# A short convolution computed from matmul banks as they fill, and one weight block rounded ahead of the first attention softmax

## The reference, cut to what matters

```python
def _short_conv_branch(b_gate, c_gate, h, conv_w, w_out):
    S = h.shape[1]
    zp = jnp.pad(c_gate * h, ((0, 0), (CONV_K - 1, 0), (0, 0)))
    y = zp[:, 0:S] * conv_w[0]
    for k in range(1, CONV_K):
        y = y + zp[:, k:k + S] * conv_w[k]
    return (b_gate * y) @ w_out
...
def _mla_branch(q_lat, kv_lat, k_rope, qn_g, kvn_g, w_uq, w_ukv, w_out, pos):
    ...
    o = _blocked_causal_attention(q, k, v, (MLA_NOPE + MLA_ROPE) ** -0.5)
    return o.reshape(Bsz, S, MLA_HEADS * MLA_V) @ w_out
```

## Time and profile before

| | |
|---|---|
| three timed runs | 2857.13, 2850.22, 2849.24 us; median 2850.22 |
| the profiled execution | 2851.05 us, of which its span from first to last instruction is 2849.2 us |
| TensorE busy | 2691.5 us, 94% of the span |
| GpSimd busy | 2204.4 us, 77% |
| ScalarE busy | 1492.1 us, 52% |
| VectorE busy | 1368.2 us, 48% |
| mean granted TensorE clock | 0.979 |

### The profile page before, as it was taken

One profiled execution on the slowest core, in us unless ns is written; L12 is line 12 of the kernel. 1 busy time (PEld: TensorE's weight loads), 2 busy tenths in 40 slices (PEclk: granted clock), 3 DMA queues, 4 the chain that ended last, 5 costly groups with the idle time before them and its releaser, 6 DMA issues.

```text
span 2849.2 us, 60006 instructions
## 1 busy us (share of the span) xinstructions
PE 2691.5 (94%) x21756; PEld 2602.7 (91%) x21756; DVE 1368.2 (48%) x2509; ACT 1492.1 (52%) x2261; POOL 2204.4 (77%) x1681
## 2 busy tenths in 40 slices
PE   8999999999999999999989989999999899898997
PEld 8998988889999989988889989998999899788997
DVE  2125445656556554535556554346433533735334
ACT  4444555465455545456465554457545644555445
POOL 8876766757978967676758968978899699667994
PEclk9999999999999999999999999999999999999998
DMA  6554434434554545443434545544555455444552
GB/s 240 184 172 150 147 134 134 156 119 156 184 170 163 185 144 174 134 148 122 168 111 163 184 140 170 185 143 160 170 184 186 137 189 182 137 135 145 190 182 79
DMA packets 123283, 452.63 MB, mean 159 GB/s; under 512 B 13680, under 2 KB 13680, under 8 KB 122480
## 3 DMA queue, kind: packets, MB, share of 16 engines
q1 hardware_dynamic: 121104, 441.43, 46.4%
q10 hardware_dynamic: 2016, 8.91, 0.9%
HBM read 449.24 MB, written 1.05 MB: 158 GB/s over the span
## 4 chain that ended last, share of the span: by engine, by line
POOL 49%; issue 24%; PE 20%; DVE 4%; ACT 1%; POOLq 1%; DVEq 0%; ACTq 0%
POOL wl L373 26%; POOL wl L374 24%; PE R L408 4%; PE R L412 4%; PE R L411 4%; PE Y L408 1%; PE Y L411 1%; PE Y L412 1%; DVE M L2276 1%; PE R L571 0%; PE Y L648 0%; DVE G L2275 0%; ACT wh L1140 0%; POOLq L379 0%; DVE XLB L1915 0%
## 5 line engine op out<-in xcount | busy, mean ns | idle before, releaser
L373 POOL TENSOR_TENSOR wl<-raw,wh 128x512 fp32r<-128x512 f32 x836 | 1114.9, 1334 | 620.3 <-ACT wh L1140 614.1
L408 PE MATMUL R<-XHB,wh 128*128 128x256 f32 (+1 forms) x4168 | 1190.7, 286 | 28.5 <-POOL wl L374 16.7
L412 PE MATMUL R<-XHB,wl 128*128 128x256 f32 (+1 forms) x4168 | 1182.2, 284 | 0.0
L411 PE MATMUL R<-XLB,wh 128*128 128x256 f32 (+1 forms) x4168 | 1178.0, 283 | 0.0
L374 POOL TENSOR_TENSOR wl<-raw,wh 128x512 fp32r<-128x512 f32 x836 | 1140.8, 1365 | 0.0
L1140 ACT ACTIVATE wh<-raw 128x1024 fp32r<-128x1024 f32 x836 | 877.3, 1058 | 287.7 <-PE R L408 206.9
L408 PEld LDWEIGHTS R<-XHB,wh 128*128 128x128 f32 x4168 | 792.1, 190 | 36.4 <-POOL wl L374 23.2
L411 PEld LDWEIGHTS R<-XLB,wh 128*128 128x128 f32 x4168 | 795.2, 191 | 1.7 <-issue 1.0
L412 PEld LDWEIGHTS R<-XHB,wl 128*128 128x128 f32 x4168 | 793.7, 190 | 0.0
L408 PE MATMUL Y<-BH,wh 128*128 128x256 f32 x1408 | 398.0, 283 | 1.3 <-DVE BL L1839 1.3
L412 PE MATMUL Y<-BH,wl 128*128 128x256 f32 x1408 | 396.4, 282 | 0.0
(11 more groups left out here) (408 smaller groups left out, 3177.9 us busy)
## 6 DMA issues: line engine op xcount, KB each, us to landing
raw<-in_stream SPq DMA_DIRECT2D x836, 512.0 KB, 3.3
G<-in_wcmp ACTq DMA_DIRECT2D x2, 2048.0 KB, 7.6
G<-in_mem ACTq DMA_DIRECT2D x2, 1024.0 KB, 6.7
TB<-in_table SPq DMA_DIRECT2D x1, 1312.0 KB, 12.4
X<-in_x SPq DMA_DIRECT2D x2, 512.0 KB, 6.0
out_dram<-X ACTq DMA_DIRECT2D x4, 256.0 KB, 2.2
WS<-in_mix_w ACTq DMA_DIRECT2D x2, 256.0 KB, 7.8
PTS<-in_mix_b ACTq DMA_DIRECT2D x2, 256.0 KB, 7.6
```

The costliest lines, as they stand in the source:

```text
L373: pool.tensor_tensor(wl[:, s, 0:512], raw[:, r, 0:512], wh[:, s, 0:512].bitcast(F32), ALU.subtract)
L408: i = pe.matmul(o, wh[w], hi, start=start, stop=False, skip_group_check=True)
L411: pe.matmul(o, wh[w], lo, start=False, stop=False, skip_group_check=True)
L412: i = pe.matmul(o, wl[w], hi, start=False, stop=stop, skip_group_check=True)
```

## The change

VectorE now makes p = c * h and the three taps directly from the bank of each h chunk, with four instructions per chunk (`convolved`): p goes into the unused half of the same bank, and the taps go from there to `Z`. The bank is given back after the fourth. ScalarE no longer evicts chunks 22 to 25. Two of the four `convolved` calls stand ahead of the token mix in VectorE's list and two behind it; the 13 old instructions behind the compressed softmax are gone. On ScalarE, one `split_next` is moved from the last gate of the first pair (`split=u != 1`) to ahead of the first pair's softmax (`ahead=1`), in latent attention alone.

```diff
-            def attention_pairs(units, filler):
+            def attention_pairs(units, filler, ahead=0):
+                for _ in range(ahead):
+                    split_next()
                 for p in range(len(units) // 2 + 1):
...
                 def z(c):
                     split_next()
+                    if Z_CH <= c < Z_CB:
+                        skip(1)
+                        return
                     m, o = chunk()
...
-                def gate(b, c):
-                    split_next()
+                def gate(b, c, split=True):
+                    if split:
+                        split_next()
...
-                attention_pairs([mla_unit(h) for h in range(8)], lambda u: (gate(u // 4, 2 * u % 8), gate(u // 4, (2 * u + 1) % 8)))
+                attention_pairs([mla_unit(h) for h in range(8)], lambda u: (gate(u // 4, 2 * u % 8), gate(u // 4, (2 * u + 1) % 8, split=u != 1)), ahead=1)
...
-                skip(UP_CHUNKS - 8 + Z_N - Z_UP - 1)
-
+                skip(UP_CHUNKS - 8)
+
+                cv = lambda k, c: col(f"conv{l}", 4 * k + c)
+
+                def convolved(c):
+                    evicted(Z_CC + c)
+                    m, o = chunk()
+                    p, y = o[:, T:2 * T], Z[:, Z_CH + c, :]
+                    step(stt(p, o[:, 0:T], col(f"b_in{l}", Z_CH + c), Z[:, Z_CC + c, :], ALU.add, ALU.mult))
+                    step(ts_(y, p, cv(2, c), None, ALU.mult))
+                    step(stt(y[:, 1:T], p[:, 0:T - 1], cv(1, c), y[:, 1:T], ALU.mult, ALU.add))
+                    take(stt(y[:, 2:T], p[:, 0:T - 2], cv(0, c), y[:, 2:T], ALU.mult, ALU.add), m)
+
+                convolved(0)
+                convolved(1)
                 for g in range(4):
                     o = ready(f"mix{g}")
...
+
+                convolved(2)
+                convolved(3)
+                skip(Z_N - Z_CB)
...
-                cv = lambda k, c: col(f"conv{l}", 4 * k + c)
-                evicted(Z_CH + 3)
-                step(tt_(Z[:, Z_CC:Z_CC + 4, :], Z[:, Z_CC:Z_CC + 4, :], Z[:, Z_CH:Z_CH + 4, :], ALU.mult))
-                for c in range(4):
-                    p, y = Z[:, Z_CC + c, :], Z[:, Z_CH + c, :]
-                    step(ts_(y, p, cv(2, c), None, ALU.mult))
-                    step(stt(y[:, 1:T], p[:, 0:T - 1], cv(1, c), y[:, 1:T], ALU.mult, ALU.add))
-                    step(stt(y[:, 2:T], p[:, 0:T - 2], cv(0, c), y[:, 2:T], ALU.mult, ALU.add))
                 evicted(Z_CB + 3)
```

## The result

The changed kernel takes 2838.49 us in the median of 5 runs (2836.86 to 2841.61), the kernel before 2853.49 in the median of 5 on the same chip (2849.24 to 2857.13): ratio 0.9949 with a 95% interval of 0.9936 to 0.9962, faster by 0.5%. The profiled execution took 2838.49 us. The forecast was 2835.4 with a range of 2830 to 2843.

A forecast was written before the change was run, and what follows sets the result against it. TensorE, busy 94%, bounds the kernel, so only its stops give time back: 7.42 us in each of two mixers, 14.8 us off 2851.05, gives 2836.2, or 2835.4 us as the median; range 2830 to 2843.

The forecast's parts named there:

- The chain: Latent attention's first pair: VectorE's convolution, ScalarE's place in line, GpSimd's remainder, then TensorE, which waits 5.22 us.
- The sum: First pair's four gate chunks, 18.99 us to 11.57: 5.22 of wait, 2.0 clock, 0.2 start; two mixers, 14.8 us.
- The new instructions: Sixteen VectorE instructions on banks, 2.1 us a chunk, 8.4 a mixer, ending ahead of the compressed scores at no cost.
- ScalarE's part: Rounding ahead of latent attention's first softmax ends at 359.2, delays exponentials 0.7 us, and readies the fourth gate block at 363.2.
- Slack 3 us: First pair's fourth gate block is ready at 363.2, and TensorE wants it at about 366.2.
- the forecast's doubled case: VectorE's three wide instructions, 3.3 us, take twice that if they meet GpSimd harder, ending at 351.6.
- clock rival: TensorE gets 1.2 GHz for a chunk here or elsewhere anyway; only waits, 10.4 us, come back: 2839.8; chance 0.07.
- the third: Bank instructions are slowed beside GpSimd; 3.4 to 5.4 us a mixer are left: 2839 to 2843; chance 0.06.
- faster: Whole kernel's median below 2841.7 us, more than 0.3% under the kernel before; chance given as 0.86.
- within 0.3%: Whole kernel's time not told from no change, 0.3% being 8.6 us; chance given as 0.11.
- The second rival: Another cause, such as its load, holds the fourth gate block; the change does nothing, 2850; chance 0.04.
- The slower rival: Late `cmp_done` holds TensorE's transposition; slower from 6.6 us a chunk, 2861 at 8 us a chunk; chance 0.03.

The follow-up runs named there:

- experiment 6: Kernel before with the convolution from SBUF, two or three of its four chunks left in the old place, no rounding ahead: 2836.85 and 2854.57 us.
- two late: Convolution from SBUF, chunks 0 and 1 at the new places, two left at the old one, no rounding ahead: 2836.85 us, ratio 0.9936 to the kernel before.
- three late: Convolution from SBUF, three of its four chunks left at the old place, no rounding ahead: 2854.57 us, ratio 1.0002 to the kernel before.
- the second set of runs: The changed kernel itself, unaltered, timed once more: 2840.85 us, ratio 0.9965 to the kernel before.
- experiment 3: Changed kernel, but ScalarE evicts chunks 22 to 25 as before and VectorE makes the convolution from SBUF at the new places: 2839.19 us, ratio 0.9951.
- experiment 2: Changed kernel without ScalarE's rounding ahead of the softmax, the convolution's part alone: 2841.01 us, ratio 0.9952.
- experiment 1: Kernel before with only ScalarE's rounding ahead of the first softmax, the convolution in its old place: 2843.42 us, ratio 0.9968.
- experiment 4: Changed kernel with each chunk's first tap instruction made 6 times (2840.83 us, ratio 0.9952) or 13 times (2864.19 us, ratio 1.0037).

## Why the prediction was right, step by step

**The chain** was right: convolution, ScalarE's place in line, GpSimd, TensorE. Experiment 6 moves its first link alone and the last follows nearly one for one: 3.48 us more lateness from two late to three, 3.22 us more wait; 1.06 more to the kernel before, 1.07 more wait.

**The sum** was 7.42 us a mixer and measured 7.41. Its parts hold too: 4.15 us of wait in experiment 6 carry 1.6 us of clock in the fourth chunk (4.47 against 2.89), as 5.22 carried 2.0. In ratio the forecast was 0.9948 to the median then at hand, 2850.22; measured is 0.9949. That the whole time agrees so closely is in part luck: the second set of runs gives 0.9965, and between the two profiled executions only 12.5 us of the pairs' 14.8 are left, because the clock fell elsewhere. The absolute forecast is 3.1 us low because the kernel before stands at 2853.49 in the larger set of runs, and the sum was brought to the median of three, 2850.22.

**The new instructions** were put at 2.1 us a chunk and take 2.05 with their gaps, ahead of the compressed scores as forecast. Here the Trainium skill (VectorE: DVE Perf Modes, Rules for kernel authors) advises a copy to SBUF where there will be many operations. Experiment 3 is that advice followed: its instructions take 807 to 964 ns in the mean against 482 to 493. The Trainium skill (SBUF - State Buffer, SBUF: two separate sides) speaks of VectorE instructions with two SBUF inputs or in a two-port mode that exclude GpSimd's. The trace agrees: the bank forms show one duration with GpSimd at work or idle, and the SBUF forms show two, 1.25 to 1.40 us beside it and 0.35 to 0.48 without it (experiment 3). Neither bears on the time of this kernel, as experiment 3 also shows.

**The step that failed: ScalarE's part.** The prediction costed the rounding ahead as part of the cure ("Slack 3 us"), and never asked what the convolution's part gives by itself. It gives everything (experiment 2). The slack was under-estimated too, 4.49, since GpSimd took 1.29 and 1.28 us there for the forecast's 3.9 in all. And what I then believed, that either half would be enough, fell in experiment 1: a rounding moved ahead hides one late block, while ScalarE's own lateness stays and meets the next pair.

**Mis-sized without effect:** the product and split, 5.9 us, within the forecast's doubled case (6.6). They now run beside GpSimd, which stood idle when they took 3.3. The chances were added up wrongly: forecast, clock rival and half of the third are 0.80 + 0.07 + 0.03 = 0.90, not 0.88, so "faster" should have had 0.88 and "within 0.3%" 0.09.

**The rivals.** The clock rival (2839.8) is refuted at its place: the pair is at 1.00, and takes 11.58 us in every profile without a wait there. It also said "or elsewhere", and 2.45 + 1.43 us of clock are lost elsewhere in the profiled execution; the second profile of the changed kernel has neither loss, so they do not follow from the change. The measured times, 15.0 and 11.7 us below the kernel before, do not decide between 14.8 and the rival's 10.4. The prediction's argument against it, that the clock is 1.00 as soon as TensorE runs on without a wait, holds only for the pairs: the compressed stretch of the kernel before has no wait and 0.90. The second rival (another cause) fell with the wait, and the third (banks slowed beside GpSimd) with the 482 to 493 ns. The slower rival has about the right total (2864 at 8.3 us a chunk for 2861 at 8) and an incomplete path: it listed `cmp_done` alone, and the token mix's banks are met first.

**What stays open:** what decides where the clock falls from one execution to the next; why three late gains nothing where its pairs gain 3 us; and whether two late, at 0.9936, is truly no slower than the changed kernel, though its pairs take 1.2 us a mixer more. The intervals overlap, and its six runs span 12.6 us.

## What to carry to other kernels

When an engine is late in a hand-ordered list, measure how late it is against the first instruction that needs it, and move work until that figure is under the slack; here 1.4 to 1.65 us of lateness is free and each microsecond over it is paid nearly in full, and behind the waits of 3 us and more measured here in clock as well. A change with two cures in it has to be costed as each alone: the one that removes the cause may make the other worthless, and the one that hides a symptom hands it to the next stage. Judge an edit of a few microseconds in 2840 by the length of the stretch in the trace, not by the whole time.

## What the runs showed of the hardware that was not expected

The granted clock falls in different places in two executions of the same instructions: 0.94 in the stretch 260 to 320 of one profile of the changed kernel, 1.00 in the other. Waits of 0.93 us, and of 2.03 us in experiment 1, are followed by a granted clock of 1.00. Those of 4.13, 4.15 and 5.22 us are followed by half the pace for a while (the next chunk 4.47 to 5.06 us for 2.89, or 0.62 over the 18 us behind the 4.13), and behind the 3.06 us in mixer 2 of experiment 4 the clock is 0.78 over the next 7.57 us, though it was at 0.66 ahead of that wait too. Stretches with small matmuls lose clock without any wait, and by one of two amounts: 17.5 us at 0.90 or 19.0 at 0.82 for the same instructions.

A VectorE instruction of 256 columns on SBUF takes 0.35 to 0.49 us while GpSimd stands idle and 1.24 to 1.50 while GpSimd works (first mixer of the kernel before and of experiments 3 and 6, two late), so its mean depends on where it stands: 807 to 964 ns with all four chunks at the early places (experiment 3), 1035 to 1339 ns with two of them at the old one (experiment 6). From a bank it is 482 to 493 ns wherever it stands.
